# A two-block transformer kernel: VectorE's order ahead of the first attention, value evictions on ScalarE, and the first weights in two transfers

## The reference, cut to what matters

```python
n = rms_norm(h, attn_norm[i]); z = n @ w_in[i]
log_a = log_sigmoid(g_low @ gla_gate_w2[i] + gla_gate_b[i]) / GLA_TAU
o_g = gla_chunked(q_g, k_g, v_g, log_a)        # chunks of 64 frames, exact pairwise decay in a chunk
o_g = rms_norm(o_g, gla_out_norm[i]) * silu(g_r)
o_m = mla_attention(q_m, k_m, v_m)             # 8 heads, block-causal softmax
h = h + concatenate([o_g, o_m]) @ w_out[i]
h = h + square(relu(rms_norm(h) @ w_mlp_up)) @ w_mlp_down
h = h + (p @ w_ple_proj) * sigmoid(rms_norm(h) @ w_ple_gate + b_ple_gate)
```

## Time and profile before

| | us |
|---|---|
| three runs | 1676.36, 1675.98, 1672.82 |
| median | 1675.98 |
| profiled execution, whole | 1674.35 |
| profiled execution, span from first to last instruction | 1672.5 |
| PE busy | 1654.6 (99%) |
| DVE busy | 941.8 (56%) |
| ACT busy | 617.2 (37%) |
| mean granted TensorE clock | 0.996 |

### The profile page before, as it was taken

One profiled execution on the slowest core, in us unless ns is written; L12 is line 12 of the kernel. 1 busy time (PEld: TensorE's weight loads), 2 busy tenths in 40 slices (PEclk: granted clock), 3 DMA queues, 4 the chain that ended last, 5 costly groups with the idle time before them and its releaser, 6 DMA issues.

```text
span 1672.5 us, 19252 instructions
## 1 busy us (share of the span) xinstructions
PE 1654.6 (99%) x8138; PEld 1343.9 (80%) x8138; DVE 941.8 (56%) x1418; ACT 617.2 (37%) x851; POOL 84.0 (5%) x81
## 2 busy tenths in 40 slices
PE   9979999999999999999999999999999999999999
PEld 7857778888888888888888888877777888888887
DVE  6677865534343456667556446655655676366353
ACT  5456534423132334533222222355654433122220
POOL 1200000000000000000000000221100200000000
PEclk9989999999999999999999999999999999999999
DMA  5210225536362522212322222322231222222211
GB/s 182 101 49 17 86 101 99 123 92 112 105 112 101 103 100 76 76 76 101 126 95 84 101 86 95 119 76 100 75 100 51 76 98 104 101 91 89 109 72 69
DMA packets 27622, 155.94 MB, mean 93 GB/s; under 512 B 3664, under 2 KB 4832, under 8 KB 11664
## 3 DMA queue, kind: packets, MB, share of 16 engines
q1 hardware_dynamic: 26064, 149.84, 25.1%
q0 software_dynamic: 1328, 4.86, 5.1%
q10 hardware_dynamic: 144, 0.00, 0.0%
HBM read 149.98 MB, written 4.72 MB: 92 GB/s over the span
## 4 chain that ended last, share of the span: by engine, by line
PE 95%; DVE 4%; ACT 0%; DMA 0%; issue 0%; POOL 0%; SPq 0%; DVEq 0%; ACTq 0%
PE bank L550 26%; PE bank L552 25%; PE bank L551 25%; PE bank L556 3%; PE bank L558 3%; PE bank L557 3%; PE bank L1145 1%; PE bank L1170 1%; PE bank L1155 1%; PE bank L765 1%; PE bank L720 1%; DVE WL L1595 1%; PE bank L811 1%; PE bank L786 0%; PE bank L1133 0%; DVE AT L1848 0%
## 5 line engine op out<-in xcount | busy, mean ns | idle before, releaser
L550 PE MATMUL bank<-AH,WH 128*128 128x512 f32 (+1 forms) x1152 | 452.6, 393 | 2.6 <-DVE X L2117 1.8
L552 PE MATMUL bank<-AH,WL 128*128 128x512 f32 (+1 forms) x1152 | 448.6, 389 | 0.0
L551 PE MATMUL bank<-AL,WH 128*128 128x512 f32 (+1 forms) x1152 | 448.4, 389 | 0.0
L1595 DVE TENSOR_TENSOR WL<-RAW,WH 128x2048 fp32r<-128x2048 f32 (+1 forms) x133 | 298.4, 2246 | 178.3 <-ACT WH L1215 178.3
L1215 ACT ACTIVATE WH<-RAW 128x2048 fp32r<-128x2048 f32 (+1 forms) x133 | 248.3, 1871 | 259.9 <-PE bank L552 240.3
L550 PEld LDWEIGHTS bank<-AH,WH 128*128 128x128 f32 (+1 forms) x1152 | 215.8, 187 | 50.6 <-issue 4.2
L552 PEld LDWEIGHTS bank<-AH,WL 128*128 128x128 f32 (+1 forms) x1152 | 215.8, 187 | 45.9
L551 PEld LDWEIGHTS bank<-AL,WH 128*128 128x128 f32 (+1 forms) x1152 | 215.9, 187 | 45.4 <-issue 1.0
L550 PE MATMUL bank<-HH,WH 128*128 128x512 f32 x608 | 239.6, 394 | 0.0
L552 PE MATMUL bank<-HH,WL 128*128 128x512 f32 x608 | 238.4, 392 | 0.0
L551 PE MATMUL bank<-HL,WH 128*128 128x512 f32 x608 | 236.0, 388 | 0.0
(11 more groups left out here) (292 smaller groups left out, 1760.5 us busy)
## 6 DMA issues: line engine op xcount, KB each, us to landing
RAW<-in_W SPq DMA_DIRECT2D x124, 1024.0 KB, 4.8
RAW<-in_W SPq DMA_DIRECT2D x9, 768.0 KB, 4.1
X<-in_XT SPq DMA_DIRECT2D x16, 256.0 KB, 3.7
ev_scratch<-ev POOLq DMA_DIRECT2D x16, 160.0 KB, 7.6
Gb<-ev_scratch SPq DMA_DIRECT2D x16, 128.0 KB, 3.9
out<-X SPq DMA_DIRECT2D x8, 256.0 KB, 2.0
Gb<-ev_scratch SPq DMA_DIRECT2D x16, 112.0 KB, 3.3
RAW<-in_W SPq DMA_DIRECT2D x3, 512.0 KB, 6.3
```

The costliest lines, as they stand in the source:

```text
L550: e.matmul(o, a, h, start=first, stop=False)
L551: e.matmul(o, a, l, start=False, stop=False)
L552: return e.matmul(o, c, h, start=False, stop=last)
L1595: e.tensor_tensor(k.WL[j][:, 0:n], k.RAW[RAW_OF[u]][:, 0:n], k.WH[j][:, 0:n].bitcast(F), SUB).then_inc(*WLO.mark(u))
```

## The change

It has these parts:

- The first half of unit 0 comes as two transfers of 384 columns (`load_piece`), the second of them behind `X` tile 1; both are split apart too. TensorE's first six products (`first_chunk`) are put in the order in which their operands come: both high by high products, both with `AL`, both with `WL`. The zero products are 9 instead of 16.
- VectorE, ahead of the attention: `fill(6)` and `fill(4)` stand ahead of and behind the two `gate` instructions, then `split(8)`, then the scans. `split(9)` goes to the end of step 0 of the attention.
- The four evictions of `gv` go to ScalarE, behind its `split(9)`.
- The first level of the triangle is written as a product of the bank and the (integer) mask into the whole of `AT`, so GpSimd's zeroing of `AT` goes away.
- `gate_part(0)` is issued ahead of step 0, there is none in step 3, and each of the others from step 4 on is one step later (the last in step 16). VectorE's evictions of them move to steps 5, 9, 13 and 17.

```diff
@@ tensor_program
+    def first_chunk():
+        a, l = first
+        tiles = ((bank[0][0:64, :], slice(0, 64)), (bank[1][:, :], slice(64, 192)))
+        w.wait_ge(k.WHI("piece", 0), ACT("ah", 0, 0))
+        for o, cols in tiles:
+            e.matmul(o, a[:, 0, cols], AH[:, 0, :], start=True, stop=False)
+        w.wait_ge(DVE("al", 0, 0))
+        for o, cols in tiles:
+            e.matmul(o, a[:, 0, cols], AL[:, 0, :], start=False, stop=False)
+        w.wait_ge(WLO("piece", 0))
+        for o, cols in tiles:
+            e.matmul(o, l[:, 0, cols], AH[:, 0, :], start=False, stop=False)
-    for _ in range(16):
+    for _ in range(ZEROS):                       # ZEROS = 9
         e.matmul(bank[7][:, 0:P], k.rb[:, 0:P], k.rb[:, 0:P], start=True, stop=True)
-    for c in range(4):
+    first_chunk()
+    for c in range(1, 4):
         low_and_values(c)
@@ gv, states
-                free[bs[q]] = [DVE("gv", q)]
+                free[bs[q]] = [ACT("gv", q)]
-        w.wait_ge(ACT("kd", j), DVE("gv", 3))
+        w.wait_ge(ACT("kd", j))
@@ attention                                    # GATED = [i for i in range(2 * MH + 1) if i != 3]
+    gate_part(0)
     for i, p, q in mla_steps():
-        if i < 4 * NT:
-            gate_part(i)
+        if i in GATED[1:]:
+            gate_part(GATED.index(i))
@@ scalar_program
-        if c == 0:
-            half_split(0, 0)
+        if c < 2:
+            piece_split(c)
...
     split(9)
+    w.wait_ge(DVE("zsum", 1, 3))
+    for q in range(NT):
+        w.wait_ge(MM("gv", 1, q))
+        e.activation(k.gv[:, q, :], bank[k.where["gv", 1, q]][:, :], AF.Copy, scale=k.r4[:, q:q + 1]).then_inc(*ACT.mark("gv", q))
@@ vector_program
     split(7)
+    fill(6)
     for j in range(2):
         w.wait_ge(ACT("gln", j))
         e.scalar_tensor_tensor(gx[j][:, :], gx[j][:, :], 0.0, ge[j][:, :], MIN, SUB).then_inc(*DVE.mark("gate", j))
-    fill(6)
+    fill(4)
+    split(8)
     for j in range(2):
         ...tensor_tensor_scan...
-    split(8)
-    fill(4)
-    split(9)
-    for q in range(NT):
-        w.wait_ge(MM("gv", 1, q))
-        e.tensor_scalar(k.gv[:, q, :], bank[where["gv", 1, q]][:, :], k.r4[:, q:q + 1], None, MUL).then_inc(*DVE.mark("gv", q))
@@ keep, level 0
-                w.wait_ge(POOL("at0"), (k.arrived["msk"], 16))
+                w.wait_ge((k.arrived["msk"], 16), WLO(UNIT["gr", 1]))
+                e.tensor_tensor(o, bank[b][:, :].rearrange("p (q n) -> p q n", q=4), m, MUL).then_inc(*DVE.mark("kept", lv, j, hh))
+                continue
@@ attention steps
-        if i % NT == 0 and 0 < i <= 4 * NT:
-            h = i // NT - 1
+        if i - 1 in GATED[3::4]:
+            h = GATED[3::4].index(i - 1)
...
             e.tensor_tensor(k.kt[:, i, :], k.gk[:, i, :], k.dd[:, i, :], MUL).then_inc(*DVE.mark("kdec", i))
+        if i == 0:
+            split(9)
@@ pool_program
-    w.wait_ge(WLO(UNIT["gr", 1]))
-    e.memset(k.AT[:, :, :], 0.0).then_inc(*POOL.mark("at0"))
@@ sync_program
     load_x(0)
-    load_half(0, 0)
-    for c in range(1, 4):
-        load_x(c)
+    load_piece(0)
+    load_x(1)
+    load_piece(1)
+    load_x(2)
+    load_x(3)
     load_half(1, 0)
```

More of the change, by code:

```diff
@@ L298, in memory @@
     k.half_in = [semaphore(f"half_in{i}") for i in range(2)]
+    k.piece_in = [semaphore(f"piece_in{i}") for i in range(2)]
     k.gb_in = [semaphore(f"gb_in{i}") for i in range(4)]
@@ L310, in half_of, with first_pieces @@
     return [z[u][:, x * n:x * n + n] for z in (k.RAW, k.WH, k.WL)] + [k.W[u, :, x * n:x * n + n]]
+def first_pieces(k, x):
+    n = PLAN[0][2] // 4
+    return [z[0][:, x * n:x * n + n] for z in (k.RAW, k.WH, k.WL)] + [k.W[0, :, x * n:x * n + n]]
 def loaded(k, u):
@@ L523, in fill_order @@
     return out + [("norm", 1, q) for q in range(NT)]
+ZEROS = 9
 def mla_steps():
     return [(i, *divmod(i, NT)) for i in range(2 * MH + 3)]
+GATED = [i for i in range(2 * MH + 1) if i != 3]
 def tensor_program(k, e):
@@ L590, in low_and_values @@
         a, l = first
-        w.wait_ge(WLO(0) if c > 3 else WLO("half", 0), DVE("al", 0, c))
+        w.wait_ge(WLO(0) if c > 3 else WLO("piece", c // 2), DVE("al", 0, c))
         t = triple(bank[0][0:64, :], a[:, c, 0:64], l[:, c, 0:64], AH[:, c, :], AL[:, c, :], c == 0, c == 7)
@@ L1239, in half_split, with piece_split @@
         e.activation(h, raw, AF.Copy).then_inc(*(WHI.mark(u) if x else WHI.mark("half", u)))
+    def piece_split(x):
+        raw, h, _, _ = first_pieces(k, x)
+        w.wait_ge((k.piece_in[x], 16))
+        e.activation(h, raw, AF.Copy).then_inc(*WHI.mark("piece", x))
     e.dma_start(par[:, 0:8], k.PV[:, 0:8]).then_inc(k.arrived["gains"], 16)
@@ L1640, in half_split, with piece_split @@
         e.tensor_tensor(l, raw, h.bitcast(F), SUB).then_inc(*(WLO.mark(u) if x else WLO.mark("half", u)))
+    def piece_split(x):
+        raw, h, l, _ = first_pieces(k, x)
+        w.wait_ge(WHI("piece", x))
+        e.tensor_tensor(l, raw, h.bitcast(F), SUB).then_inc(*WLO.mark("piece", x))
     e.memset(rb[:, 0:P], 0.0).then_inc(*DVE.mark("still"))
@@ L1835, in keep @@
             b, h = (7, 3)[hh], 2 * j + hh
+            w.wait_ge(MM("level", lv, j, hh))
             if lv == 0:
@@ L1838, in keep @@
                 m = k.msk[:, 0, None, :].to_broadcast([P, 4, P])
-                d = bank[b][:, :].rearrange("p (q n) -> p q n", q=4)
-                w.wait_ge(POOL("at0"), (k.arrived["msk"], 16))
[L1841 to L1847, removed]
+                w.wait_ge((k.arrived["msk"], 16), WLO(UNIT["gr", 1]))
+                e.tensor_tensor(o, bank[b][:, :].rearrange("p (q n) -> p q n", q=4), m, MUL).then_inc(*DVE.mark("kept", lv, j, hh))
+                continue
+            B = LEVELS[lv - 1]
+            o = k.AT[:, h, :].rearrange("p (q n w) -> p q n w", q=4, w=2 * B)[:, :, :, B:2 * B]
+            m = k.msk[:, lv, :].rearrange("p (n w) -> p n w", w=2 * B)[:, None, :, B:2 * B].to_broadcast([P, 4, 64 // B, B])
+            d = bank[b][:, 0:256].rearrange("p (q n w) -> p q n w", q=4, w=B)
+            w.wait_ge(DVE("kept", lv - 1, j, hh))
             e.copy_predicated(o, m, d).then_inc(*DVE.mark("kept", lv, j, hh))
@@ L2350, in load_half, with load_piece @@
         e.dma_start(raw, src).then_inc(*((k.raw_full[u], 16) if x else (k.half_in[u], 16)))
+    def load_piece(x):
+        raw, _, _, src = first_pieces(k, x)
+        e.dma_start(raw, src).then_inc(k.piece_in[x], 16)
     load_x(0)
-    load_half(0, 0)
-    for c in range(1, 4):
-        load_x(c)
+    load_piece(0)
[3 more added lines that the diff above has]
+    load_x(3)
     load_half(1, 0)
```

## The result

The changed kernel takes 1661.74 us (median of 4 runs, 1661.16 to 1663.08), against 1674.46 for the kernel before (4 runs, 1672.82 to 1676.36; a fourth, of 1672.94, came after the prediction): ratio 0.9923, interval 0.9912 to 0.9935. The profiled execution took 1662.28, span 1660.4.

A forecast was written before the change was run, and what follows sets the result against it. TensorE, busy 1654.6 of 1672.5 us, was taken as the bound. Profiled 1674.35 less 10.8 (entry and steps 0 to 3) and 1.3 (start) gives 1662.2; with half the median's difference, 1663.0, range 1659.5 to 1667.5.

The forecast's parts named there:

- The entry: Entry of the first attention: new VectorE order and ScalarE evictions bring first scores at 98.0 against 107.77, -9.8 us.
- Steps 0 to 3: First attention steps: gate moves gain, `split(9)` costs about 0.35; -10.85 us in all at the first level.
- The masked product: First level of the triangle: product with the mask costs the same as masked copies, 0; GpSimd's zeroing simply goes.
- The start: Opening stretch: smaller first transfer lets TensorE start at 5.6 and reach `low_queries` at 11.8 against 13.05, -1.3 us.
- The zero products: Opening: 9 instead of 16 might keep the clock low; start then worth -0.3 or costing 1.4; -1.3 kept.
- rival 1: Opening stretch: the clock stays low at the start, total 1664 to 1665.7 us; chance 0.25.
- The clock at 212: Low-clock stretch at 212 to 216, cost 1.0 us: may not recur or last longer; 0 taken, 1.7 either way.
- From the sum to the forecast: Total: half the 1.6 us by which the runs' median exceeded the profiled execution is added, 1662.2 to 1663.0.

The follow-up runs named there:

- e3: Kernel before with only the four `gv` evictions moved to ScalarE, VectorE's order as before; 1671.60 us, ratio 0.9984.
- e4: Kernel before with only VectorE's new order, `gv` still evicted by VectorE, `gate_part(0)` and masked copy as before; 1670.74 us, ratio 0.9978.
- e1: Changed kernel with the start of the kernel before (one transfer, 16 zero products, old chunk 0 order); 1662.34 us, ratio 0.9931 to the kernel before.
- e9: Kernel of e3 plus 21 products of 512 columns that nobody reads, in front of the third head; 1667.26 us, ratio 0.9953 to the kernel before.
- e5: Changed kernel with the output-gate products in the steps where they were; 1662.75 us, ratio 0.9921 to the kernel before.
- e6: Changed kernel with the masked copy and GpSimd's zeroing of `AT` kept; 1665.76 us, ratio 0.9948 to the kernel before.
- e8: Changed kernel with unit 1's second half split ahead of `X` tile 7's parts, on ScalarE and VectorE; 1662.79 us, ratio 0.9926 to the kernel before.
- e2: Kernel before with only the new start (two pieces, 9 zero products, new chunk 0 order); 1674.33 us, ratio 1.0001.
- e12: Changed kernel measured once more, on the chip of e6, e8 and e11; 1663.37 us, ratio 0.9931 to the kernel before.
- e10: Kernel before with 38 products that nobody reads in front of its heads, filling the 9.1 us wait; 1673.49 us, ratio 0.9985.
- e7: Changed kernel with the first half of unit 0 in one transfer of 768 columns, still split in two pieces; 1661.86 us, ratio 0.9916 to the kernel before.
- e11: Changed kernel with one transfer for unit 0's first half, 12 zero products, unit 1's second half split earlier; 1660.87 us, ratio 0.9920 to the kernel before.

## Why the prediction came out right, step by step

- **The entry** (forecast 9.8, measured 9.97). The order was read rightly job by job: maxima of step 0 forecast 98.8, seen 98.80; heads at 94.6, seen 94.69; ScalarE's last eviction starts at 94.89, forecast 94.7. Here e3 and e4 teach more than the total. Alone the evictions bring 2.6 us, alone the order 3.5, both with gate and mask 11.9 (e1). Each alone leaves a wait of 5.25 or 3.64 us, in and behind which the clock is at its low level for 8 us or more; in e3 that took 3.1 us, which e9 gives back. Three other things are in the difference: the gate's move, 0.5 (e5); the zeroing beside VectorE's division, which e4 still has; and the low stretch of 1.5 us, which the profiles of e3 and e4 have (e4 at 190 us) and that of e1 hasn't. No run has the two parts and nothing else. An estimate from the traces, by the distance from the last `gv` product to the first out-sum products (before 116.9, e6 109.15) less 0.5 for the gate: together 7.3 us, alone 2.3 and 1.8 (3.4 without e4's low stretch). That is how a change can be worth more than its parts.
- **Steps 0 to 3** (forecast 10.85 in all at the first level, measured 10.78 from the last `gv` product). `split(9)`, now at the end of step 0, is felt as 0.29 us before the scores of step 2, forecast 0.3 to 0.35. The wait for ScalarE's copy in step 3 is 0.78, forecast 0.8. The gate's move is worth 0.5 by e5; I had put 0.65 for step 3, less 0.1 for step 16.
- **The masked product** (forecast 0): right for the operation, 1.29 against 1.35 us, and wrong for the whole edit. I wrote of GpSimd's zeroing only that it goes. I hadn't asked what it would have run beside once `split(9)`, which releases it, stood in step 0. e6 prices it at 2.4 us by the medians and 3.05 by the traces: 1.4 for the wait, the rest behind it, at the low clock. The sum holds only because the change takes the zeroing out together with the move.
- **The start** (forecast -1.3, measured +0.2): the step that failed is that the half of unit 1 is ready at 11.75, as before, and that "everything from there to 94.6 is paced by TensorE, with no wait over 0.5 us". TensorE got to `low_queries` at 11.2, earlier than the 11.8 forecast, but the half of unit 1 had moved too: ScalarE took it up at 9.73 instead of 9.42, the wait for its transfer ending 0.3 later, and TensorE stood for 0.72. Then the second half of unit 1, split behind tile 7's part at 18.78 (before 17.34), stopped it for 0.82 at 20.05. For the extra issue on SyncE's queue I had allowed a loss of 0.4 us in the range and none in the sum. All profiles together tell more than one pair: with two transfers ScalarE takes the half of unit 1 up at 9.57 to 9.95 (six profiles, mean 9.76), with one at 8.91 to 9.72 (eight, mean 9.28). SyncE issues that transfer at 3.55 instead of 3.07, the same 0.48 later. Whether the issue does it, or the transfers that share the engines, no run tells. The second wait goes with the order of the splits (e8), but it isn't there in e5 and e6 either. The last `gv` product starts at 93.44 to 94.46 with the new start (after, e2, e5, e6, e12; mean 93.9) and at 93.81 to 94.56 with the old one (before, e1, e3, e4, e9, e10; mean 94.2): it is worth 0.2 us on average, less than the scatter of either, and the profile after is the latest of its five.
- **The zero products** (rival 1, 0.25): not in this kernel. Five other profiles with this start (e2, e5, e6, e8, e12) have 0.34 to 0.54 us between the zero products and the first real one, the profile after almost nothing, and all are at full pace by 7.1. The rival came in e7, with 0.76 us between. My "until about 9.5" was right to the tenth, though the median shows no price for it: there are no waits for unit 1 in that kernel.
- **The clock at 212** (forecast 0, within 1.7): -1.54 in the profile. My price of 1.0 us for the stretch came from the row of 212 to 216 alone; the next one, 216 to 220, has 0.83 and belongs to it. The same kernel shows the stretch in e12 and not in the first profile. Two errors, 1.5 at the start and 1.5 here, cancelled: that 12.1 came out to the tenth is luck. With the low stretch the profiled execution would have taken 1662.28 + 1.54 = 1663.8, near e12's 1663.37, and still lie in the range, which needed no luck.
- **From the sum to the forecast** (1662.2 to 1663.0): the 0.8 was half of what the median of three runs lay above the profiled one. The fourth run brought that median from 1675.98 to 1674.46, 0.1 above the profiled 1674.35; the addition had no ground, and it was small.

## What to carry to other kernels

Where TensorE is the bound, remove all causes of a long wait together: half a removal can leave a wait with a low clock behind it, and that eats the gain (3.1 us in e3). A job that you move takes with it what it releases: look on which other engine that starts something, and beside what. And what comes earlier at the start is worth only as much as the next thing due behind it.

## What the runs showed of the hardware that I had not expected

- A GpSimd memset of 128 x 2048 (1.80 us) and VectorE's `tensor_scalar` from SBUF to SBUF, begun 0.06 us behind it, ended together: the latter took 1.90 us instead of 0.48 (e6, and e4 with 1.91).
- A stretch at 1.2 GHz worth 1.5 to 1.6 us wherever it comes: from 214 to 217 in before and between 200 and 208 in e12, with TensorE busy throughout (4.00 of 4.00 us), about 190 in e4 behind a short wait, nowhere in the profiles after and of e1, e5, e7, e9, e10 or e11. What decides is open: one kernel shows it in one profile and not in another.
- Behind 18 zero-product records a gap of 0.76 us went with 3.5 us of products at half pace (e7); one of 0.54 did not (e8), nor did 0.38 behind 24 (e11). Each is one profile, so that the gap is the cause isn't shown.
